# Attention of layer 1 in a two-layer decoder trunk: other distances between the steps of a head group, nine early pieces of the output projection, table loads only at a change of set

## The chip, the cores and the metric

The kernel runs on one core of a Trainium2 chip. The metric is the device time of one execution in microseconds; lower is better. DVE is VectorE, ACT is ScalarE, PE is TensorE, PEld its weight loads, SP the engine that issues the weight transfers.

## The reference

Two layers over 256 positions, width 2048, all in float32. Layer 0 mixes with gated DeltaNet heads and RG-LRU channels, layer 1 with banded attention; each layer then has cross attention to 256 memory tokens and a gated feed-forward part. What the change touches is the mixer of layer 1:

```
q, k, v = split(h @ swa_in_w)           # 32 query heads, 8 key/value heads, 64 wide
q = rope(rmsnorm(q) * q_norm);  k = rope(rmsnorm(k) * k_norm)
s = q k^T / 8 over the own and the previous block of 128, masked to a band of 128
m = max(max(s), sink);  p = exp(s - m) / (sum(exp(s - m)) + exp(sink - m))
x = x + (p v) @ swa_out_w
```

## The kernel before, in words

All weights stream once from memory, in 800 pieces of 512 x 256 numbers. A piece goes through four steps: a transfer into `w_raw` (SP), a cast to its high part `w_hi` on ACT (`split`, L475), the rest `w_lo` on DVE (`split`, L875), and 24 matmuls of 128x256 on PE (`piece`, L1460 to L1462; in the feed-forward input `wide_piece`). Each buffer holds four pieces, and ACT and DVE split three pieces ahead (`AHEAD`): in tick t they split piece t + 3, and that cast waits until PE has done piece t - 1. Four pieces give a group of 256 output columns.

Each engine has its own program, written by hand as a list of ticks. A tick is one piece and after it (on PE) or after its split (on ACT and DVE) the other work of this tick. Engines meet only through semaphores, and each runs its list strictly in order. So the order on every engine, and with it what waits behind what, is set by the tick at which a step is put.

In layer 1 the keys and values take 16 ticks (`SWKV`) and the queries 32 (`SWQ`), four ticks for one group g of four query heads. The attention of group g is a chain of steps at ticks 4g + lag (`swa_first`, `swa_side`, `rope`):

| step of group g | engine, line | lag before | lag after |
|---|---|---|---|
| take the group out of PSUM, square | DVE L884, ACT L541 | 3 | 3 |
| sum over the head | PE L1690 | 4 | 4, behind the scores |
| table load, logarithm, exponential (root) | ACT L478, L548, L549 | 4 | 4, mostly no load |
| refine the root, normalise ("normalising") | DVE L888 to L890, L1339 | 5 | 5 |
| rotation matmul | PE L1866 | 6 | 7 |
| last step of the rotation | DVE L1343 to L1345 | 6 | 7, ahead of L884 |
| scores | PE L1907, L1908 | 7 | 8 |
| mask and maxima | DVE L1371 to L1384 | 7 | 8 |
| exponentials | ACT L805 to L807 | 8, ahead of the root | 9 |
| scale by the row sums ("scaling") | DVE L1352 to L1355 | 9, ahead of the split | 10, behind it |
| transposes | PE L1444 | 10 | 11 |
| copies of them | ACT L823 | 10 | 11 |
| product with V | PE L1890 to L1892 | 11 | 12 |
| split of the output into `act` ("output split") | DVE L901, L902 | 12 | 13 |

The steps of the last groups run on into the output projection (`common(1)`, `mixout`). Its piece (g, q) needs the attention of the groups up to 2q + 1. `mix_order` and `EARLY` give the order of its first pieces: those that need the last groups least come first. A group's accumulator lies in one of two banks by turns (`ST`); a third one can lie in bank `B[1]`, which is free once the last queries are rotated.

`tables(name)` on ACT loads a set of activation tables, at every call. Logarithm and exponential are in one set, which `head_rstd`, `row_rstd` and parts of layer 0's mixer ask for; in layer 0's projection the chain at tick 9 is: sums on PE (L1561), load, four table functions (L573 to L576), cast, `w_lo`, then `q_buf`, `k_buf`, `k_dec` on DVE (L1028 to L1033) for the matmuls of tick 11 (L1554).

Of the kernel before, what the change touches and what calls it, by code (L numbers as in the profile page):

```python
# [80 lines left out]
EARLY = [(0, 0), (0, 1), (0, 2), (1, 0), (1, 1), (1, 2), (0, 3), (1, 3)]  # L81
# [11 lines left out]
def mix_order(layer, t):  # L93

    return EARLY[t] if layer and t < 8 else (t // 4, t % 4)

# [73 lines left out]
def trunk(nc, a, out):  # L170
    ctx = ExitStack()
    with ctx:
# [287 lines left out]
        def _(act):  # L460
# [15 lines left out]

            def tables(name):
                nc.scalar.preload_act_table_set(name)  # L478
# [218 lines left out]
            def common(layer):  # L697
# [7 lines left out]
                if layer == 1:  # L705
                    for t in range(32, 41):
                        if t < 38:
                            mixout(t - 32)
                        swa_first(t)
                        swa_side(t)  # L710
                    first = 6
# [87 lines left out]
            def swa_first(t):  # L799

                g = (t - 8) // 4
                if 8 <= t and g < 8 and t == 4 * g + 8:
                    act.wait_ge(s_neg, g + 1)
                    for i in range(4):
                        f(sc[:, i, 0:P], sc[:, i, 0:P], ACT.Exp, bias=sst[:, 1, i:i + 1], accum_out=sst[:, 2, i:i + 1])  # L805
                        f(sc[:, i, P:384], sc[:, i, P:384], ACT.Exp, bias=sst[:, 1, 4 + i:5 + i], accum_out=sst[:, 2, 4 + i:5 + i])  # L806
                    f(sst[:, 4, :], sst[:, 3, :], ACT.Exp).then_inc(s_exp, 1)  # L807

            def swa_side(t):

                g = (t - 3) // 4
                if 3 <= t and g < 8 and t - 4 * g == 3:
                    swa_rope(N_ROPE + 2 + g, GROUP[SWQ] + g, 3)
                g = (t - 4) // 4
                if 4 <= t and g < 8 and t == 4 * g + 4:
                    swa_rope(N_ROPE + 2 + g, 0, 4)
                g = (t - 10) // 4
                if 10 <= t and g < 8 and t == 4 * g + 10:
# [5 lines left out]
                    last.then_inc(pt_copied, 1)  # L824

# [14 lines left out]
            for t in range(16):  # L840
# [6 lines left out]
                if t in (7, 11):  # L847
                    act.wait_ge(ksw_done, g)
                    nc.scalar.copy(kTs[:, 2 * (g - 1):2 * g, :], B[2][:].rearrange("p (k c) -> p k c", k=2)).then_inc(ksw_ready, 1)
                if t == 12:  # L850
                    act.wait_ge(svT, 1)
                    nc.scalar.copy(vtok[:, :, 0:2, :], B[0][:].rearrange("p (t k c) -> p t k c", t=TT, k=2)).then_inc(sv_ready, 1)
            for t in range(32):
                split(SWQ + t + AHEAD)
                swa_first(t)
# [584 lines left out]
        def _(pe):  # L1440
# [492 lines left out]
            for t in range(16):  # L1933
# [12 lines left out]
                if t == 12:  # L1946
                    swa_v(0)
# [27 lines left out]
```

## Time and profile before

| | |
|---|---|
| times of three runs | 2801.35, 2809.43, 2815.41 us; median 2809.43 |
| profiled execution: time, span | 2811.95 us, 2809.8 us |
| mean granted clock of PE | 0.975 of full |
| chain that ended last, by engine | PE 82%, DVE 10%, ACT 5%, issue 2%, DMA 1% |
| table loads | 54, 69.3 us on ACT |
| keys and queries of layer 1 up to the first late piece of the output projection | about 1595 to 1884 us |

The span is that of the instructions on the core, the time that of the whole execution. The clock row is the mean of what the chip granted to PE: full speed is 2.4 GHz, half is 1.2.

### The profile page before, as it was taken

Reading aid. Unit: us, or ns where it says so; the run is one execution under the profiler, and the core shown is the slowest. Engines: PE = TensorE matmul, PEld = TensorE weight load, DVE = VectorE, ACT = ScalarE, POOL = GpSimd, SP = SyncE. Lnnn points to the kernel's source line nnn. Section 1 sums busy time; section 2 is a strip of 40 time slices with the busy share of each in tenths; the row PEclk is TensorE's granted clock in tenths of the full one; section 3 lists DMA queues with packets and bytes.
Section 4 is the critical chain, followed back from the end, with each engine's and each line's share of the span. In section 5 each row is a group of like instructions: output and inputs, shape, how many; then the busy total and the mean of one; then the engine's idle time right before and its main releaser. Section 6 shows DMA issues by size and latency. Waiting matters only on the chain.

```text
span 2809.8 us, 46427 instructions
## 1 busy us (share of the span) xinstructions
PE 2658.7 (95%) x18376; PEld 2455.4 (87%) x18376; DVE 1789.3 (64%) x2468; ACT 1169.4 (42%) x1490; POOL 10.0 (0%) x18
## 2 busy tenths in 40 slices
PE   6898998899899999999999998789899999999999
PEld 5798898899898899889989886679788998899889
DVE  4666666655777755775576656655577746764774
ACT  2434434444444433443444444433444434443443
POOL 0000000000000000000000000000000000000000
PEclk8999999999999999999999999889899999999999
DMA  5343443355446655565555442225256655665554
GB/s 149 99 120 99 114 119 108 111 167 163 144 146 188 192 186 180 184 189 187 181 185 180 152 128 83 76 80 172 87 166 193 189 184 173 189 193 184 183 182 155
DMA packets 429633, 432.62 MB, mean 154 GB/s; under 512 B 15487, under 2 KB 427796, under 8 KB 429108
## 3 DMA queue, kind: packets, MB, share of 16 engines
q1 hardware_dynamic: 422832, 422.63, 48.6%
q0 software_dynamic: 1584, 5.40, 0.7%
q10 hardware_dynamic: 5076, 2.56, 0.3%
q8 instruction: 107, 1.75, 0.3%
q14 instruction: 34, 0.28, 0.0%
HBM read 428.44 MB, written 2.10 MB: 153 GB/s over the span
## 4 chain that ended last, share of the span: by engine, by line
PE 82%; DVE 10%; ACT 5%; issue 2%; DMA 1%; SPq 0%; ACTq 0%; POOL 0%; DVEq 0%
PE stream L1475 23%; PE stream L1460 13%; PE stream L1461 12%; PE stream L1462 12%; PE stream L1476 12%; DVE w_lo L875 2%; PE bank L1554 1%; ACT w_hi L475 1%; PE bank L1495 1%; ACT L478 1%; PE bank L1444 1%; PE bank L1866 1%; PE stream L1554 1%; DMA cst<-in_consts 1%; ACT scores L806 0%
## 5 line engine op out<-in xcount | busy, mean ns | idle before, releaser
L875 DVE TENSOR_TENSOR w_lo<-w_raw,w_hi 128x1024 fp32r<-128x1024 f32 x800 | 965.8, 1222 | 585.8 <-ACT w_hi L475 582.3
L475 ACT CAST w_hi<-w_raw 128x1024 fp32r<-128x1024 f32 x800 | 833.9, 1047 | 822.0 <-PE stream L1462 481.0
L1475 PE MATMUL stream<-h,w_hi 128*128 128x512 f32 x2816 | 992.2, 398 | 0.0
L1476 PE MATMUL stream<-h,w_lo 128*128 128x256 f32 x2816 | 788.9, 280 | 0.0
L1475 PEld LDWEIGHTS stream<-h,w_hi 128*128 128x128 f32 x2816 | 529.0, 188 | 130.2
L1460 PE MATMUL stream<-act,w_hi 128*128 128x256 f32 x2048 | 589.6, 288 | 2.6 <-DVE act L902 2.5
L1462 PE MATMUL stream<-act,w_lo 128*128 128x256 f32 x2048 | 581.1, 284 | 0.0
L1461 PE MATMUL stream<-act,w_hi 128*128 128x256 f32 x2048 | 581.1, 284 | 0.0
L1476 PEld LDWEIGHTS stream<-h,w_lo 128*128 128x128 f32 x2816 | 531.4, 189 | 0.1
L1460 PE MATMUL stream<-h,w_hi 128*128 128x256 f32 x1536 | 472.8, 308 | 3.0 <-DVE w_lo L875 3.0
L1461 PE MATMUL stream<-h,w_hi 128*128 128x256 f32 x1536 | 444.5, 289 | 0.0
L1462 PE MATMUL stream<-h,w_lo 128*128 128x256 f32 x1536 | 443.7, 289 | 0.0
L1460 PEld LDWEIGHTS stream<-act,w_hi 128*128 128x128 f32 x2048 | 394.8, 193 | 6.5 <-DVE act L902 3.9
L1461 PEld LDWEIGHTS stream<-act,w_hi 128*128 128x128 f32 x2048 | 394.6, 193 | 1.6 <-issue 0.8
L1462 PEld LDWEIGHTS stream<-act,w_lo 128*128 128x128 f32 x2048 | 394.5, 193 | 0.0
L1460 PEld LDWEIGHTS stream<-h,w_hi 128*128 128x128 f32 x1536 | 306.2, 199 | 19.1 <-issue 15.3
L1461 PEld LDWEIGHTS stream<-h,w_hi 128*128 128x128 f32 x1536 | 305.5, 199 | 10.1 <-issue 9.6
L1462 PEld LDWEIGHTS stream<-h,w_lo 128*128 128x128 f32 x1536 | 304.6, 198 | 0.0
L1231 DVE TENSOR_TENSOR ffn_cross<-stream,ffn_cross 128x512 f32<-128x512 f32 x88 | 60.9, 692 | 99.0 <-ACT ffn_cross L765 99.0
L765 ACT COPY ffn_cross<-stream 128x512 f32<-128x512 f32 x88 | 51.6, 587 | 155.4 <-PE stream L1476 155.4
L478 ACT ACT_TABLE_LOAD x54 | 69.3, 1283 | 60.7 <-PE bank L1600 29.8
L929 DVE SCALAR_TENSOR_TENSOR ffn_conv<-ffn_pad,par,ffn_conv 128x256 f32<-128x256 f32 x176 | 77.6, 482 | 13.1 <-DVE ffn_conv L923 6.7
(332 smaller groups left out, 1741.0 us busy)
## 6 DMA issues: line engine op xcount, KB each, us to landing
w_raw<-in_ffn_in_w SPq DMA_DIRECT2D x352, 512.0 KB, 4.5
w_raw<-in_ffn_out_w SPq DMA_DIRECT2D x176, 512.0 KB, 3.6
w_raw<-in_hyb_in_w SPq DMA_DIRECT2D x96, 512.0 KB, 3.8
w_raw<-in_swa_in_w SPq DMA_DIRECT2D x48, 512.0 KB, 3.5
w_raw<-in_xkv_w SPq DMA_DIRECT2D x32, 512.0 KB, 3.5
w_raw<-in_hyb_out_w SPq DMA_DIRECT2D x32, 512.0 KB, 3.5
w_raw<-in_swa_out_w SPq DMA_DIRECT2D x32, 512.0 KB, 3.4
w_raw<-in_xq_w SPq DMA_DIRECT2D x16, 512.0 KB, 3.5
```

What stands on the lines that cost most here:

```text
L475: nc.scalar.copy(whi[:, k], raw[:, n % NRAW]).then_inc(hi_split, 1)
L478: nc.scalar.preload_act_table_set(name)
L765: nc.scalar.copy(two(frt[:, t // 4]), wide(g0 + t // 4)[:, :, TOK:512]).then_inc(ffn_right, 1)
L875: v.tensor_tensor(wlo[:, k], raw[:, n % NRAW], whi[:, k].bitcast(F32), ALU.subtract).then_inc(lo_split, 1)
L929: last = v.scalar_tensor_tensor(d, pad[:, b, j:j + TOK], par[:, col(j, b)], d, ALU.mult, ALU.add)
L1231: v.tensor_tensor(two(frt[:, t // 4]), both[:, :, 0:TOK], two(frt[:, t // 4]), ALU.add).then_inc(group_evac, 1)
L1460: mm(o, whi[:, k, kk, w], src[:, kt, 0, :], start=first, stop=False, skip_group_check=True)
L1461: mm(o, whi[:, k, kk, w], src[:, kt, 1, :], start=False, stop=False, skip_group_check=True)
L1462: last = mm(o, wlo[:, k, kk, w], src[:, kt, 0, :], start=False, stop=final, skip_group_check=True)
L1475: mm(bank[:, m, :], whi[:, k, kk, w], h[:, kt, :, :], start=(q == 0 and kk == 0), stop=False, skip_group_check=True)
L1476: last = mm(bank[:, m, 0:TOK], wlo[:, k, kk, w], h[:, kt, 0, :], start=False, stop=(q == 3 and kk == len(kts) - 1), skip_group_check=True)
L1554: last = mm(bank[:, s], lhs[:, s], rhs if rhs.shape[1] == P else rhs[:, s], start=True, stop=True)
```

## The change

The attention steps after the normalising move one tick later each, in the keys' ticks too, and change their order within a tick; the row scaling goes behind the split and ahead of the next mask. `EARLY` takes nine pieces of three groups instead of six of two, the third group in `B[1]`. The tail of the attention runs to tick 41 instead of 40. `tables` loads only if the name differs from the last one: 26 loads instead of 54.

```diff
-EARLY = [(0, 0), (0, 1), (0, 2), (1, 0), (1, 1), (1, 2), (0, 3), (1, 3)]
+EARLY = [(g, q) for g in range(3) for q in range(3)] + [(g, 3) for g in range(3)]
+SWA_LAST = 42
...
             def tables(name):
-                nc.scalar.preload_act_table_set(name)
+                if loaded[0] != name:
+                    nc.scalar.preload_act_table_set(name)
+                loaded[0] = name
...
             def swa_side(t):
+                for lag in (7, 3, 5):
+                    g = (t - lag) // 4
+                    if t >= lag and g < 8 and t == 4 * g + lag:
+                        if lag == 7 and g:
+                            dve.wait_ge(s_done, g)
+                        rope(lag, N_ROPE + 2 + g, GROUP[SWQ] + g, SWQ + t, two(qf[:]), "swa_q_norm", q_rot)
+                g = (t - 10) // 4
+                if t >= 10 and g < 8 and t == 4 * g + 10:
                     dve.wait_ge(s_exp, g + 1)
...
-                g = (t - 7) // 4
-                if 7 <= t and g < 8 and t == 4 * g + 7:
+                g = (t - 8) // 4
+                if t >= 8 and g < 8 and t == 4 * g + 8:
                     dve.wait_ge(s_done, g + 1)
...
-                if t == 6:
+                if t == 7:
                     pe.wait_ge(n_out, ni + 1)
                     mm(B[1][:], c_("rot"), nraw[:], start=True, stop=True).then_inc(rot_done, 1)
...
-                    piece(MIXOUT[layer] + t, GROUP[MIXOUT[layer]] + g, q, 3, act_, range(NK * q, NK * q + NK))
+                    third = layer and g == 2
+                    if third and q == 0:
+                        pe.wait_ge(q_rot, 8)
+                    piece(MIXOUT[layer] + t, GROUP[MIXOUT[layer]] + g, q, 3, act_, range(NK * q, NK * q + NK), B[1] if third else None)
...
-                g = (t - 12) // 4
-                if 12 <= t and g < 8 and t == 4 * g + 12:
+                g = (t - 13) // 4
+                if t >= 13 and t == 4 * g + 13:
                     dve.wait_ge(pv_done, g + 1)
```

First place: DVE in the middle of the queries, from the `w_lo` behind the maxima on. The names are tiles, `softmax_small` and `scores` of the scaling, `norm_sq`, `norm_r`, `norm_raw` of the next group's normalising, `act` the output split. Before:

```order
L875 TENSOR_TENSOR w_lo<-w_raw,w_hi 128x1024
L901 CAST act<-stream 128x2x256
L902 TENSOR_TENSOR act<-stream,act 128x2x256
L1352 TENSOR_TENSOR softmax_small<-softmax_small 128x8
L1353 RECIPROCAL softmax_small<-softmax_small 128x8
L1354 TENSOR_TENSOR scores<-scores,softmax_small 128x4x128
L1355 TENSOR_TENSOR scores<-scores,softmax_small 128x4x256
L875 TENSOR_TENSOR w_lo<-w_raw,w_hi 128x1024
L888 SCALAR_TENSOR_TENSOR norm_sq<-bank,norm_r 128x512
L889 SCALAR_TENSOR_TENSOR norm_sq<-norm_sq,norm_r 128x512
L890 SCALAR_TENSOR_TENSOR norm_r<-norm_sq,norm_r 128x512
L1339 SCALAR_TENSOR_TENSOR norm_raw<-norm_raw,par,norm_r 128x512
```

The change:

```order
L875 TENSOR_TENSOR w_lo<-w_raw,w_hi 128x1024
L888 SCALAR_TENSOR_TENSOR norm_sq<-bank,norm_r 128x512
L889 SCALAR_TENSOR_TENSOR norm_sq<-norm_sq,norm_r 128x512
L890 SCALAR_TENSOR_TENSOR norm_r<-norm_sq,norm_r 128x512
L1339 SCALAR_TENSOR_TENSOR norm_raw<-norm_raw,par,norm_r 128x512
L901 CAST act<-stream 128x2x256
L902 TENSOR_TENSOR act<-stream,act 128x2x256
L875 TENSOR_TENSOR w_lo<-w_raw,w_hi 128x1024
L1357 TENSOR_TENSOR softmax_small<-softmax_small 128x8
L1358 RECIPROCAL softmax_small<-softmax_small 128x8
L1359 TENSOR_TENSOR scores<-scores,softmax_small 128x4x128
L1360 TENSOR_TENSOR scores<-scores,softmax_small 128x4x256
```

The normalising and the output split now both stand ahead of the scaling, and the `w_lo` that stood between scaling and normalising is now ahead of the scaling.

Second place: ACT in the same turn, from the end of the exponentials (`softmax_small`) on; `norm_r` is the root, `probsT` the copies of the transposes, `norm_sq` the square of a new group. Before:

```order
L807 ACTIVATE softmax_small<-softmax_small 128x8
L478 ACT_TABLE_LOAD
L548 ACTIVATE norm_r<-bank,bias_consts 128x512
L549 ACTIVATE norm_r<-norm_r 128x512
L475 CAST w_hi<-w_raw 128x1024 x2
L823 COPY probsT<-bank 128x512 x2
L823 COPY probsT<-stream 128x512
L475 CAST w_hi<-w_raw 128x1024
L541 ACTIVATE norm_sq<-norm_raw 128x512
L475 CAST w_hi<-w_raw 128x1024
```

The change:

```order
L825 ACTIVATE softmax_small<-softmax_small 128x8
L476 CAST w_hi<-w_raw 128x1024 x2
L811 COPY probsT<-bank 128x512 x2
L811 COPY probsT<-stream 128x512
L546 ACTIVATE norm_sq<-norm_raw 128x512
L476 CAST w_hi<-w_raw 128x1024
L553 ACTIVATE norm_r<-bank,bias_consts 128x512
L554 ACTIVATE norm_r<-norm_r 128x512
L476 CAST w_hi<-w_raw 128x1024
```

The root has moved from ahead of the copies to behind the square, and the load in front of it is gone.

Third place: DVE in the keys' ticks, from the normalising of a key group on. Before:

```order
L1339 SCALAR_TENSOR_TENSOR norm_raw<-norm_raw,par,norm_r 128x512
L875 TENSOR_TENSOR w_lo<-w_raw,w_hi 128x1024
L1343 TENSOR_TENSOR norm_sq<-bank,sin 128x512
L1344 TENSOR_TENSOR norm_raw<-norm_raw,cos 128x512
L1345 TENSOR_TENSOR kT<-norm_raw,norm_sq 128x512
L875 TENSOR_TENSOR w_lo<-w_raw,w_hi 128x1024
L884 TENSOR_TENSOR norm_raw<-stream,rstd 128x512
```

The change:

```order
L1339 SCALAR_TENSOR_TENSOR norm_raw<-norm_raw,par,norm_r 128x512
L875 TENSOR_TENSOR w_lo<-w_raw,w_hi 128x1024 x2
L1343 TENSOR_TENSOR norm_sq<-bank,sin 128x512
L1344 TENSOR_TENSOR norm_raw<-norm_raw,cos 128x512
L1345 TENSOR_TENSOR kT<-norm_raw,norm_sq 128x512
L884 TENSOR_TENSOR norm_raw<-stream,rstd 128x512
```

The last step of the rotation (`kT`) has moved behind one more `w_lo` and now stands directly ahead of the next group's `norm_raw`.

## Rows read from the trace of the kernel before

**Rows 1.** The page's first part: busy time, share of the span, instructions.
```profile
PE 2658.7 (95%) x18376; PEld 2455.4 (87%) x18376; DVE 1789.3 (64%) x2468; ACT 1169.4 (42%) x1490; POOL 10.0 (0%) x18
```

**Rows 2.** Waits of TensorE, 1590 to 1890: line waited for, total us, times, longest.
```profile
PE bank L1866 <- DVE norm_raw L1339: 33.2, 10, 3.9
PE bank L1444 <- DVE scores L1355: 9.9, 8, 4.5
PE stream L1890 <- ACT probsT L823: 1.7, 1, 1.7
PE stream L1460 <- DVE act L902: 1.5, 1, 1.5
```

**Rows 3.** Windows: length, busy of PE, PEld, DVE, ACT, POOL; clock, DMA share, GB/s.
```profile
1595.50:1648.00 52.50, 48.45 (x347) 44.79 (x346) 28.99 (x33) 21.18 (x25) 0.00 (x0) 0.93 0.50 157
1685.40:1711.70 26.30, 21.56 (x152) 18.65 (x152) 17.73 (x26) 12.17 (x29) 0.00 (x0) 0.94 0.27 81
...
1738.00:1765.40 27.40, 22.68 (x152) 19.56 (x152) 17.73 (x26) 12.11 (x29) 0.00 (x0) 0.88 0.26 77
```

**Rows 4.** Timeline of TensorE, one turn: start, length, what [idle before, releaser].
```profile
1737.97 1.09 PE L1444 MATMUL bank<-cst,scores 128*128 128x128 f32 x8 [0.82 <-DVE scores L1355]
...
1743.38 2.07 PE L1866 MATMUL bank<-norm_raw,cst 128*128 128x512 f32 x2 [3.88 <-DVE norm_raw L1339]
...
1750.01 0.43 PE L1890 MATMUL stream<-probsT,v_tok 128*64 128x128 f32 x2
...
1751.74 0.48 PE L1907 MATMUL bank<-kT_swapped,q_rot 64*128 64x128 f32 x2
...
1757.85 1.02 PE L1690 MATMUL bank<-norm_sq,cst 128*128 128x512 f32 x2
```

**Rows 5.** Timeline of DVE, the same turn.
```profile
1735.65 0.17 DVE L1352 TENSOR_TENSOR softmax_small<-softmax_small 128x8 f32<-128x8 f32 x1 [1.32 <-ACT softmax_small L807]
...
1740.40 0.68 DVE L888 SCALAR_TENSOR_TENSOR norm_sq<-bank,norm_r 128x512 f32<-128x512 f32 x1
...
1754.98 0.69 DVE L1371 SCALAR_TENSOR_TENSOR scores<-bank,cst 128x512 f32<-128x512 f32 x1 [4.10 <-PE stream L1908]
...
1759.24 1.22 DVE L875 TENSOR_TENSOR w_lo<-w_raw,w_hi 128x1024 fp32r<-128x1024 f32 x1
1760.38 0.68 DVE L901 CAST act<-stream 128x512 fp32r<-128x512 f32 x1
```

**Rows 6.** Timeline of ACT, the same turn.
```profile
1731.90 0.41 ACT L805 ACTIVATE scores<-scores,softmax_small 128x128 f32<-128x128 f32 x1 [6.88 <-DVE softmax_small L1384]
...
1735.64 1.28 ACT L478 ACT_TABLE_LOAD   x1
...
1738.19 1.98 ACT L475 CAST w_hi<-w_raw 128x1024 fp32r<-128x1024 f32 x2
```

**Rows 7.** Instructions of line 478: duration ns min, median, max, first and last start.
```profile
L478 ACT ACT_TABLE_LOAD  x54: 1283/1283/1283, 40.9 to 2056.8; - x54
```

**Rows 8.** Layer 0's projection: waits of TensorE; timelines of ACT and DVE.
```profile
PE bank L1554 <- DVE k_dec L1033: 9.5, 4, 2.4
...
446.06 1.28 ACT L478 ACT_TABLE_LOAD   x1 [0.22 <-PE bank L1561]
...
450.87 1.22 DVE L875 TENSOR_TENSOR w_lo<-w_raw,w_hi 128x1024 fp32r<-128x1024 f32 x1 [2.12 <-ACT w_hi L475]
```

**Rows 9.** Windows of one microsecond, columns as in rows 3.
```profile
223.00:224.00 1.00, 1.00 (x10) 1.00 (x9) 0.74 (x1) 0.00 (x0) 0.00 (x0) 0.78 0.82 289
...
454.00:455.00 1.00, 0.84 (x7) 0.84 (x8) 1.00 (x2) 0.00 (x0) 0.00 (x0) 1.00 1.00 348
1991.00:1992.00 1.00, 1.00 (x5) 0.83 (x6) 0.93 (x1) 0.00 (x0) 0.00 (x0) 0.83 0.01 3
```

**Rows 10.** Layer 1's cross attention: timelines of TensorE and DVE.
```profile
1990.85 3.03 PE L1714 MATMUL bank<-kv_mem,xq 128*128 128x256 f32 x8 [2.02 <-DVE xq L1188]
...
2003.74 0.69 DVE L888 SCALAR_TENSOR_TENSOR norm_sq<-bank,norm_r 128x512 f32<-128x512 f32 x1 [0.83 <-ACT norm_r L549]
```

More of the change, by code:

```diff
@@ L93, in mix_order @@
 def mix_order(layer, t):
-    return EARLY[t] if layer and t < 8 else (t // 4, t % 4)
+    return EARLY[t] if layer and t < len(EARLY) else (t // 4, t % 4)
 CONST = {}
@@ L797, in swa_rope @@
                     head_rstd(ni, B[0][:], nr[:], SWA_HD)
[L799 to L807, printed above, removed]
-            def swa_side(t):
[L811 to L818, printed above, removed]
+            def swa_side(t):
+                g = (t - 11) // 4
+                if t >= 11 and t == 4 * g + 11:
                     act.wait_ge(pt_done, g + 1)
@@ L824, in swa_side @@
                     last.then_inc(pt_copied, 1)
+                g = (t - 3) // 4
+                if g < 8 and t == 4 * g + 3:
+                    swa_rope(N_ROPE + 2 + g, GROUP[SWQ] + g, 3)
+                g = (t - 4) // 4
+                if t >= 4 and g < 8 and t == 4 * g + 4:
+                    swa_rope(N_ROPE + 2 + g, 0, 4)
+                g = (t - 9) // 4
+                if t >= 9 and g < 8 and t == 4 * g + 9:
+                    act.wait_ge(s_neg, g + 1)
+                    for i in range(4):
+                        f(sc[:, i, 0:P], sc[:, i, 0:P], ACT.Exp, bias=sst[:, 1, i:i + 1], accum_out=sst[:, 2, i:i + 1])
+                        f(sc[:, i, P:384], sc[:, i, P:384], ACT.Exp, bias=sst[:, 1, 4 + i:5 + i], accum_out=sst[:, 2, 4 + i:5 + i])
+                    f(sst[:, 4, :], sst[:, 3, :], ACT.Exp).then_inc(s_exp, 1)
             for t in range(16):
@@ L854, in _ @@
                 split(SWQ + t + AHEAD)
-                swa_first(t)
                 if t == 0:
@@ L1259, in mixout @@
                     if q == 3:
-                        residual(GROUP[MIXOUT[layer]] + g, g, MIXOUT[layer] + t, "norm_cross", KT * layer)
+                        residual(GROUP[MIXOUT[layer]] + g, g, MIXOUT[layer] + t, "norm_cross", KT * layer,
+                                 B[1] if layer and g == 2 else None)
                 first = 0
                 if layer == 1:
-                    for t in range(32, 41):
-                        swa_first(t)
-                        if t < 38:
+                    for t in range(32, SWA_LAST):
+                        if t < 41:
                             mixout(t - 32)
                         swa_side(t)
-                    first = 6
+                    first = 9
                 for t in range(first, 32):
@@ L1763, in common @@
                         mem_side(0, 16)
-                    g = {7: 0, 8: 1}.get(t) if layer and t <= 8 else t // 4 - 1 if t % 4 == 0 and t else None
+                    g = {10: 0, 11: 1, 12: 2}.get(t) if layer and t <= 12 else t // 4 - 1 if t % 4 == 0 and t else None
                     if g is not None:
```

84 lines of the change are left out of this document (39 added, 45 removed).

## The prediction, made before the change was run

> **What bounds the kernel now.** The page's first part comes first: TensorE is busy 95% of the span [rows 1]. So time can only come from its 5% of idle, from stretches at half clock, or from other engines where they make it wait. The waits of TensorE in the stretch of layer 1's attention (1590 to 1890 us) say where [rows 2]. It waits 33.2 us in 10 places for the normalised heads ahead of the rotation (L1866), 9.9 us in 8 places for the scaled scores ahead of their transposes (L1444), and 1.7 and 1.5 us at the end. Seven of the ten L1866 waits are 3.88 (queries 1 to 7), which leaves 2.0 for each of the other three (two groups of keys, first group of queries). So the eight groups of queries with their end hold 33.2 - 6.1 + 9.9 + 1.7 + 1.5 = 40.2 us of waiting.
>
> The windows by group give the second loss, the clock [rows 3]. A group takes 26.3 us at a mean clock of 0.94 or 27.4 at 0.88. At half of full clock work takes twice as long, so (1 - clock) x length is lost: 1.6 or 3.3 us. I take 2.9 for the latter, since part of that low stretch falls into the wait itself. Two groups lose 1.6 and six (the last with the end) about 2.9: 20.6 us.
>
> The timelines of the three engines give one turn of the loop, counted from the end of the scores of a group (DVE starts the mask at 1754.98) [rows 4 to 6]. TensorE: a piece until 1757.85, so 2.9; head sum 1.0; transposes 1737.97 to 1739.50 (the wait's 3.88 ahead of 1743.38), so 1.5; rotation about 1.0 at full clock; product with V 1750.01 to 1751.74, 1.7; scores until the mask at 1754.98, 3.2. DVE: mask, maxima 1754.98 to 1759.24, 4.3; w_lo 1.14; normalising 1740.40 to the rotation at 1743.38, 2.9 and the hand-over; output split two operations of 0.68, 1.4; scaling 1735.65 to the transposes at 1737.97, 2.3; last step of the rotation three operations of this size (0.69, as at 1754.98), 2.0. ACT: exponentials 1731.90 to 1735.64, 3.75; table load 1.28; logarithm and exponential until 1738.19, 1.3; a cast 1.0.
>
> The old loop checks this. Mask, exponentials, scaling: 4.3 + 3.75 + 2.3 = 10.4. From 1737.97 to 1740.40 DVE waits for a cast that sits behind the table load and does a w_lo, 2.4, then the normalising, 3.0. Then rotation, piece, V, scores: 1.0 + 2.9 + 1.7 + 3.2 = 8.8. Sum 24.6; with 1.6 or 2.9 of clock 26.2 or 27.5. The windows show 26.3 and 27.4 [rows 3].
>
> **The change, part by part.**
>
> *Table loads.* 54 loads become 26; each of the 54 took 1283 ns, although most load the set that is in place [rows 7]. Of the 28 removed, those count that end a wait of TensorE. In layer 0's projection TensorE waits 2.4 us four times for k_dec [rows 8]. The load at 446.06 starts as soon as TensorE's sums are there, then come four table functions and the cast, and DVE has waited 2.12 for that cast at 450.87. All of it moves up by the load: 4 x 1.28 = 5.1. Two of these four waits were followed by half clock (at 223 us, and so in the third pair), two were not (454 us) [rows 9]. A rest of 1.1 should bring none, 2 x 1.7 = 3.4 more. In layer 1's cross attention the wait of 2.02 at 1990.85 shrinks by 1.28, and the fall of the clock at 1991 (1.7, [rows 9]) should go too; the next chain gains only the 0.8 for which DVE waited for ACT at 2003.74 [rows 10]. Together 3.8. The other removed loads lie beside running pieces: 0; a cover gone would show as a wait ahead of a piece.
>
> The Trainium skill (ScalarE: Activation LUTs, "What ACT_TABLE_LOAD costs") puts 1283 ns plus a drain of about 1380 ns on each switch to another set. By the rows load, logarithm and exponential together take 2.55 (1735.64 to the casts at 1738.19) [rows 6], which leaves no room for such a drain; by the page the four places would give up to their whole wait, 9.5 instead of 5.1.
>
> *Rotation a step later (keys and first queries).* TensorE reaches the rotation after one more piece, 2.9 against a wait of 2.0: all 6.1 us go, and the half clock that followed two of them: 0.93 over 52.5 us is 3.7 lost [rows 3], of which I take 3.4. New: the evacuation of the next group now stands behind the rotation's last step on DVE. The square on ACT (0.63) then ends 2.0 + 0.7 + 0.6 = 3.3 after the rotation, TensorE asks for it after one piece, 2.9: 0.5 lost, once. Sum 9.0. Later groups have the scores in between and lose nothing.
>
> *The queries' loop.* New order on DVE from the end of the scores: mask 4.3, w_lo 1.14, normalising 2.9 (its input from ACT is there at 1.0 + 1.3 = 2.3, wanted at 5.4), output split 1.4, w_lo 1.14 (its cast is behind the exponentials, 4.3 + 3.75 + 1.0 = 9.1, wanted at 9.7), scaling 2.3. The transposes can start at 13.2. TensorE has 1.0 + 3 x 2.9 = 9.7 of work, so it waits 3.5. The rotation behind them no longer waits, since its input was ready at 8.3. From there 1.5 + 1.0 + 2.9 + 1.7 + 3.2 = 10.3: a turn of 23.5 against 24.6. On DVE behind the scaling: w_lo, rotation's last step, evacuation, w_lo; the last waits for its cast, which stands behind square and copies on ACT. It ends about 21.1, so 2.4 of room before the mask at 23.5. On ACT the head's square ends about 18.9, wanted at 23.5.
>
> The waits of the eight groups: group 0 has no output split, but then DVE waits for the cast: 12.6 - 9.7 = 2.9. Groups 1 to 5: 5 x 3.5 = 17.5. Group 6: the third mix-output piece (1, or (0,2)) is the first to need the output split of group 5, which DVE reaches at 9.8, while TensorE is there after 1.0 + 2.9: a wait of 5.9, and none at its transposes. Group 7: no normalising, scaling done at 12.6; TensorE has three pieces, 8.7: 3.9. That is where the pieces of the early third group lie: they fill what were waits of 4.5 and 1.7 with nothing in them. At the end one more output split: 1.5. Sum 31.7 against 40.2: 8.5 gained.
>
> The clock behind these waits was not seen for this arrangement. A wait of 3.88 was followed by one low stretch (1.7) twice and by two (2.9) five times [rows 3]. Those had a shorter wait and the transposes ahead of them, which here stand behind. I take 2.2 for each of six, and 5.6 for group 6 and the end: 18.8 against 20.6, 1.8 gained; the bounds are 1.7 and 2.9 for each of the six (15.8 and 23.0): +4.8 to -2.4.
>
> The Trainium skill (TensorE: Matmul & The Clock Gate, "Part 4: PE-mode transpose") says that transposes do not count as busy for the clock the way matmuls do, which speaks against this order. By it, wait and transposes are one quiet stretch of 5.0, each group loses 2.9, and the loop gains 6.1 instead of 10.3.
>
> *Sum.* 5.1 + 3.4 + 3.8 + 9.0 + 8.5 + 1.8 = 31.6 us. The profiled execution took 2811.95 for its span of 2809.8, so 2780 there. The median of the three runs is 2.5 lower, 2809.4; I forecast 2779.
>
> **The rivals.** Half a per cent, 14 us, is about what a measurement of this kernel tells from no change.
>
> 1. The forecast, a gain of 24 to 40 us: 2770 to 2786. Chance 0.60.
> 2. The queries' loop gives nothing: DVE's work in front of the scaling (4.3 + 1.14 + 2.9 + 1.4 + 1.14 = 10.9, where mask and exponentials took 8.1) leaves a turn only 1.1 us shorter, and more falls of the clock in two steps, or hand-overs that I left out of the walk, eat that. For it: five of seven such waits had two steps. Against: one of the two waits of a turn goes whole. 31.6 - 10.3 = 21.3, or 18 if the clock of layer 0 stays as it is: 2788 to 2792. Chance 0.22.
> 3. Loads and loop give nothing, the chains being held by something else that comes at the same time; only the steps of the keys are left, 9.0: 2800. Against: DVE's wait for the cast is 2.12 long in the row. Chance 0.09.
> 4. More than 40 us, if most falls of the clock behind 3.5 us go: 2760 to 2769. Chance 0.04.
> 5. Slower, over 2823. The normalising now stands ahead of the scaling on DVE's queue and waits for ACT's root of the next group. If that is late, the scaling, the transposes and the whole turn are late. It has 5.4 - 2.3 = 3.1 us of room. To undo the 21 us made elsewhere and lose 14 more, seven turns must each lose 6.5 against my walk (35 + 10.3 over seven): the root 9.6 us late. ACT's work ahead of it (copies, square, cast) ends 4 us before it is wanted. Chance 0.05.
>
> Within 0.5%: rival 3 and a tenth of rival 2, 0.11. Slower 0.05, faster the rest, 0.84. The range 2762 to 2800 takes in cases 1, 2 and most of 4.
>
> **What the profile after would show.** Table loads 26. L1866's waits for norm_raw gone (under 1 us in all). TensorE's wait for the scaled scores longest with 3.5 in six groups, starts of those transposes 25 to 26.5 apart instead of 27.4. A wait of about 5.9 ahead of a piece for DVE's act. k_dec's wait 4 x 1.1. The window 1600 to 1648 at a clock near 1. The forecast is wrong if the transposes stay 27 apart, if w_lo turns up as a releaser of TensorE, or if new falls of the clock appear where there was none.

## The result and the profile after

The changed kernel takes 2777.77 us (median of 4 runs, 2772.21 to 2782.40) against 2809.76 for the kernel before on the same chip (4 runs, 2801.35 to 2815.41): ratio 0.988, interval 0.985 to 0.991. Timed again beside the experiments it took 2776.19, ratio 0.986 (0.983 to 0.989). The forecast was 2779.

So the gain was 32.0 us the first time and 40.3 us the second (2816.53 - 2776.19). The profiled executions, 2811.95 and 2772.21, lie 39.7 us apart, since the one after is the fastest of its four. I use its rows for places and shapes, and keep the second profile of the same kernel (2776.19, span 2772.9) beside it where a size matters.

The page's first two lines of after, to be read with [rows 1]:

```profile
span 2770.0 us, 46406 instructions
...
PE 2643.6 (95%) x18376; PEld 2446.2 (88%) x18376; DVE 1788.6 (65%) x2468; ACT 1134.3 (41%) x1462; POOL 10.0 (0%) x18
```

The same 18376 matmuls are there. Span minus busy time gives TensorE's idle time: 151.1 before (2809.8 - 2658.7), 126.4 after. So, between the two profiles, 24.7 us less is waiting, and 15.1 us less is matmuls that ran for less time. These are the two terms of the forecast, waits (21.3) and clock (10.3), read for the whole kernel from one row. I use this ledger for every experiment.

One part of the 15.1 has nothing to do with the change. Count the matmuls in order of their starts: from the 5601st to the 6801st (828.9 to 1029.1 us before) TensorE never waits and the granted clock is 1.00, yet they took 200.2 us before and 196.9 after. The two profiles of the loads-only kernel below, one and the same program, show 200.2 and 196.9 as well. So 3.3 us of TensorE's busy time come and go between executions; why is open.

The waits of TensorE from 1560 to 1895, the stretch of [rows 2]:

```profile
PE bank L1440 <- DVE scores L1360: 23.4, 7, 3.7
PE stream L1456 <- DVE act L902: 7.3, 2, 5.8
...
PE bank L1686 <- issue: 1.0, 1, 1.0
```

No row names `norm_raw` any more: where it cost 33.2 us, the transposes now wait 23.4. One turn of the loop on the three engines, to be laid beside [rows 4 to 6] (start, length, what, idle time before it and its releaser). TensorE:

```profile
1717.79 1.97 PE L1440 MATMUL bank<-cst,scores 128*128 128x128 f32 x8 [3.36 <-DVE scores L1360]
...
1720.40 1.91 PE L1865 MATMUL bank<-norm_raw,cst 128*128 128x512 f32 x2
...
1743.68 1.71 PE L1440 MATMUL bank<-cst,scores 128*128 128x128 f32 x8 [3.36 <-DVE scores L1360]
...
1815.52 0.58 PE L1456 MATMUL stream<-act,w_hi 128*128 128x256 f32 x1 [5.81 <-DVE act L902]
...
1845.56 1.22 PE L1440 MATMUL bank<-cst,scores 128*128 128x128 f32 x8 [3.74 <-DVE scores L1360]
```

DVE and ACT in the same turn:

```profile
1730.67 0.69 DVE L1368 SCALAR_TENSOR_TENSOR scores<-bank,cst 128x512 f32<-128x512 f32 x1 [2.66 <-PE stream L1908]
...
1736.07 0.68 DVE L888 SCALAR_TENSOR_TENSOR norm_sq<-bank,norm_r 128x512 f32<-128x512 f32 x1
...
1742.41 1.22 DVE L1360 TENSOR_TENSOR scores<-scores,softmax_small 128x1024 f32<-128x1024 f32 x1
...
1731.73 0.69 ACT L553 ACTIVATE norm_r<-bank,bias_consts 128x512 f32<-128x512 f32 x1 [4.97 <-PE bank L1686]
```

The mask starts at 1730.67 and the transposes at 1743.68, 13.0 apart (walked: 13.2). Between them DVE never waits: no instruction of it from 1731.28 to 1742.41 has a bracket, the two shown at 1736.07 and 1742.41 among them. The root is taken at 1731.73, 1.1 after the mask starts, so rival 5 (a late root in front of the scaling) has its 3 us of room. The waits of 5.81 and 3.74 are those walked for groups 6 and 7.

The turns by windows, with the columns of [rows 3]; the clock is the first figure behind POOL:

```profile
1584.00:1636.50 52.50, 51.45 (x400) 48.39 (x399) 31.00 (x35) 23.36 (x27) 0.00 (x0) 1.00 0.58 176
1693.16:1717.79 24.63, 21.21 (x152) 18.82 (x153) 17.64 (x27) 10.99 (x27) 0.00 (x0) 0.92 0.27 85
1717.79:1743.68 25.89, 22.47 (x152) 19.60 (x153) 17.64 (x27) 11.00 (x27) 0.00 (x0) 0.89 0.27 84
1743.68:1768.53 24.85, 21.43 (x153) 18.72 (x153) 17.64 (x27) 10.99 (x27) 0.00 (x0) 0.92 0.27 85
1768.53:1793.02 24.49, 21.07 (x153) 18.76 (x153) 17.63 (x27) 10.99 (x27) 0.00 (x0) 0.92 0.28 86
```

The keys (first row) run at full clock; before they had 0.93. The turn ahead of the four had no low stretch and took 23.17 us (transposes at 1669.99 and 1693.16; walked: 23.5). The four shown took 24.5 to 25.9, so the half clock cost each of them 1.3 to 2.7 us.

In layer 0 the waits for `k_dec` and the loads:

```profile
PE bank L1550 <- DVE k_dec L1033: 3.3, 3, 1.1
...
L482 ACT ACT_TABLE_LOAD x26 | 33.4, 1283 | 38.7 <-PE bank L1596 29.8 <-DVE angle L1413 4.0 <-PE bank L1491 3.2
```

9.5 in four [rows 8] are now 3.3 in three, and 54 loads [rows 7] are 26. The second profile has all four waits:

```profile
PE bank L1550 <- DVE k_dec L1033: 4.4, 4, 1.1
```

The clock behind the two of these waits that half clock had followed, in windows of 5 us from the end of the wait. Before:

```profile
222.66:227.66 5.00, 5.00 (x30) 5.00 (x31) 1.08 (x1) 0.00 (x0) 0.00 (x0) 0.66 0.60 186
339.20:344.20 5.00, 5.00 (x30) 5.00 (x31) 1.07 (x1) 0.00 (x0) 0.00 (x0) 0.66 0.61 188
```

After:

```profile
223.73:228.73 5.00, 5.00 (x44) 5.00 (x45) 2.20 (x5) 0.00 (x0) 0.00 (x0) 1.00 0.60 182
335.90:340.90 5.00, 5.00 (x44) 5.00 (x45) 2.21 (x5) 0.00 (x0) 0.00 (x0) 1.00 0.62 191
```

### The profile page after: what moved, and what is told of

The parts are those of the page before. It is cut to its first block and busy times, and to the rows that moved or that the text cites. A ratio compares the mean times of both kernels' runs of the same rounds, so it can differ in the third digit from the quotient of the medians.

```text
span 2770.0 us, 46406 instructions
## 1 busy us (share of the span) xinstructions
PE 2643.6 (95%) x18376; PEld 2446.2 (88%) x18376; DVE 1788.6 (65%) x2468; ACT 1134.3 (41%) x1462; POOL 10.0 (0%) x18
## 5 line engine op out<-in xcount | busy, mean ns | idle before, releaser
L1456 PE MATMUL stream<-act,w_hi 128*128 128x256 f32 x2016 | 581.0, 288 | 8.3 <-DVE act L902 8.3
L1458 PE MATMUL stream<-act,w_lo 128*128 128x256 f32 x2016 | 572.3, 284 | 0.0
L1457 PE MATMUL stream<-act,w_hi 128*128 128x256 f32 x2016 | 572.3, 284 | 0.0
L1456 PE MATMUL stream<-h,w_hi 128*128 128x256 f32 x1536 | 464.7, 303 | 3.0 <-DVE w_lo L875 3.0
L1457 PE MATMUL stream<-h,w_hi 128*128 128x256 f32 x1536 | 439.9, 286 | 0.0
L1456 PEld LDWEIGHTS stream<-act,w_hi 128*128 128x128 f32 x2016 | 389.0, 193 | 11.9 <-DVE act L902 9.5
L1457 PEld LDWEIGHTS stream<-act,w_hi 128*128 128x128 f32 x2016 | 388.8, 193 | 1.8 <-issue 1.0
L1458 PEld LDWEIGHTS stream<-act,w_lo 128*128 128x128 f32 x2016 | 388.6, 193 | 0.0
L1456 PEld LDWEIGHTS stream<-h,w_hi 128*128 128x128 f32 x1536 | 301.2, 196 | 15.7 <-issue 11.9
L1193 DVE TENSOR_TENSOR xT<-stream,xT 128x512 f32<-128x512 f32 x79 | 54.6, 691 | 47.3 <-PE stream L1458 47.2
```

The costliest lines, as they stand in the source:

```text
L1193: v.tensor_tensor(x2, two(ST[gi % 2] if bank is None else bank), x2, ALU.add).then_inc(group_evac, 1)
L1456: mm(o, whi[:, k, kk, w], src[:, kt, 0, :], start=first, stop=False, skip_group_check=True)
L1457: mm(o, whi[:, k, kk, w], src[:, kt, 1, :], start=False, stop=False, skip_group_check=True)
L1458: last = mm(o, wlo[:, k, kk, w], src[:, kt, 0, :], start=False, stop=final, skip_group_check=True)
```

## The experiments

They ran in three sets, each beside the kernel before on the same chip (2815.66, 2816.53 and 2812.25 us; 15, 11 and 11 runs). "Idle" and "busy" are TensorE's, against 151.1 and 2658.7 before, from the first two lines of each page. They come from one execution each, and the kernel before has one profile only: two profiles of one kernel differ by up to 3 us in them, and medians are safer for totals. Where two kernels of different sets are compared, I compare what each gained on the kernel before of its own set, since that reference moved by 4 us.

| kernel | median us | ratio (interval) | idle | busy |
|---|---|---|---|---|
| the change, again | 2776.19 | 0.986 (0.983 to 0.989) | -22.1 | -14.8 |
| loads only | 2768.99 | 0.983 (0.982 to 0.984) | -23.2 | -19.8 |
| loads only, again | 2768.27 | 0.984 (0.981 to 0.986) | -21.3 | -22.8 |
| the queries' 7 loads only | 2782.15 | 0.989 (0.987 to 0.992) | -9.4 | -17.2 |
| steps only | 2794.00 | 0.993 (0.991 to 0.994) | -7.2 | -10.8 |
| keys' step only | 2808.02 | 0.997 (0.996 to 0.998) | -0.4 | -1.5 |
| loads and keys' step | 2765.62 | 0.984 (0.981 to 0.986) | -23.5 | -15.9 |
| the change, old early list | 2776.62 | 0.986 (0.985 to 0.988) | -20.4 | -16.3 |
| the change, other early order | 2773.46 | 0.985 (0.983 to 0.988) | -25.2 | -17.2 |
| that, scaling first | 2738.43 | 0.973 (0.971 to 0.976) | -46.8 | -32.0 |
| scaling first, all loads | 2751.62 | 0.980 (0.977 to 0.983) | -31.3 | -30.1 |
| scaling first, output split ahead of it | 2752.91 | 0.979 (0.976 to 0.982) | -35.7 | -23.4 |

### The two halves of the change

Loads only is the kernel before with the memory of the last set:

```diff
             def tables(name):
-                nc.scalar.preload_act_table_set(name)
+                if loaded[0] != name:
+                    nc.scalar.preload_act_table_set(name)
+                loaded[0] = name
```

> The kernel before with the table loads only at a change of set (54 loads become 26), nothing else. Theory A: loads cost wherever ACT's chain is what TensorE waits for, and in the old order of the queries' loop that holds in every turn, since the cast for which DVE waits ahead of the normalising stands behind the load: 7 x 1.3, plus 3 x 1.3 at the rotations of the keys and of the first queries, plus 5.1 in layer 0's projection, plus 2.1 in the cross attention: about 20 us, 2788 to 2792, and the wait for norm_raw falls from 33.2 to about 20. Theory B (the account of the prediction, which counts the loads outside the loop alone and gives the loop to the steps): 5.1 + 3.8, up to 3.4 of clock, 2797 to 2802. Theory C: loads are hidden everywhere, no change.

Steps only is the changed kernel with a load at every call again.

> The changed kernel with a table load at every call again (54). Theory A: in the new order the load of a turn stands on ACT where nothing waits for it, so the keys give 9 and the queries' loop and the end 10 as walked: 2788 to 2792, and the two halves of the change add up to more than the whole (32 us). Theory B: the halves add up, 32 less what the loads give alone (9 to 12): 2786 to 2789. If the load does end a wait in the new loop, turns of more than 25 us between transposes: 2795 or more.

The loads alone make 2768.99, below everything that was expected of them and below the whole change. The expected waits came (23.2 us less idle, against about 20); what no theory had is the 19.8 us of matmul time. The steps alone make 2794.00, above both theories (2786 to 2792) and just under the mark for a load that ends a wait in the new loop. The waits of the loads-only kernel from 1560 to 1895:

```profile
PE bank L1870 <- DVE norm_raw L1343: 20.6, 10, 2.5
PE bank L1448 <- DVE scores L1359: 9.9, 8, 4.5
```

33.2 has become 20.6. A turn there, on ACT and DVE:

```profile
1714.49 0.19 ACT L811 ACTIVATE softmax_small<-softmax_small 128x8 f32<-128x8 f32 x1
1714.59 0.67 ACT L552 ACTIVATE norm_r<-bank,bias_consts 128x512 f32<-128x512 f32 x1
...
1715.76 1.22 DVE L1359 TENSOR_TENSOR scores<-scores,softmax_small 128x1024 f32<-128x1024 f32 x1
1716.90 1.22 DVE L879 TENSOR_TENSOR w_lo<-w_raw,w_hi 128x1024 fp32r<-128x1024 f32 x1
1718.03 0.68 DVE L892 SCALAR_TENSOR_TENSOR norm_sq<-bank,norm_r 128x512 f32<-128x512 f32 x1
```

The root follows the exponentials at once, and `w_lo` and the normalising follow the scaling without a gap. Before, load, root and cast ended behind the scaling, and DVE stood 1.34 us in front of that `w_lo`:

```profile
1739.26 1.23 DVE L875 TENSOR_TENSOR w_lo<-w_raw,w_hi 128x1024 fp32r<-128x1024 f32 x1 [1.34 <-ACT w_hi L475]
```

So the load in the loop was on the path: it is in the 2.4 us from 1737.97 to 1740.40 of the old walk, and TensorE's wait of 3.88 is 2.44 without it.

Both were run again in one set, to see whether loads only really beats the change.

> The kernel before with table loads only at a change of set once more, beside the changed kernel. Theory A: 0.983 again, some 10 to 15 us below the changed kernel, because the old order without the load has turns of 25.0 (a wait of 2.5 ahead of the rotation, seldom followed by half clock), the new one turns of 24.5 to 25.9 and a wait of 5.8 at the end. Theory B: the same time as the changed kernel within 0.3%.

> The changed kernel once more, on the chip and in the rounds of the next three. Theory A (the steps of the queries' loop take back a part of what the loads give): ratio to the kernel before about 0.988, clearly above the loads alone. Theory B (the kernel with the loads alone came out low by its run): both within 0.3% of each other.

It does, by 7.9 us (2768.27 against 2776.19). That is less than the 10 to 15 of theory A and, at 0.29%, just inside the 0.3% of theory B, so the two expectations don't decide it. The single times do better: all six of loads only lie below four of the change's five. In the first set the loads-only kernel (2764.20 to 2771.91) also lies wholly below the change with its old early list (2772.79 to 2779.13). The ledger says where: the idle time is the same (-21.3 and -22.1), the busy time is 8.0 us lower. The steps of the change thus cost nothing in waiting on top of the loads, and 8 us in matmul time.

### The loads of the queries alone

The kernel before, with no load at the roots of queries 1 to 7:

```diff
             def head_rstd(ni, bank, dst, width):
...
-                tables(LN_EXP)
+                if not 9 <= ni <= 15:
+                    tables(LN_EXP)
```

> The kernel before without the seven table loads of queries 1 to 7; the other 47 stay. Theory: each turn loses the 1.3 us for which DVE waited for the cast behind the load, 9.4 in all, and the shorter wait ahead of the rotation (2.5 instead of 3.9) is followed by fewer low stretches, 20.6 down to 8 to 11 of clock: 19 to 22 us, half of what all 28 loads give. Rival (the loads matter outside the loop): 9 us or less.

Seven loads, 9.0 us of ACT's time, are worth 30.1 us by the medians (23 to 37 by the interval), where 19 to 22 were expected. The waits for `norm_raw` fall from 33.2 to 23.2, which is 7 times 1.44, and that is the 9.4 of idle time. Busy time is 17.2 less, but not all of it belongs to these loads. By windows of one microsecond the queries lose 12.2 us less to half clock (20.6 to 8.4), which with the waits makes 22, as expected. Another 5.3 us is in the cross attention (8.6 to 3.3), whose loads this kernel leaves in place, and counts as chance.

```profile
PE bank L1867 <- DVE norm_raw L1340: 23.2, 10, 2.4
```

Now the change can be added up, roughly. Loads alone give 46.7 us (48.3 the second time), of which the loop has 22 to 30, so the others give 17 to 25. The steps alone give 21.7. Together 39 to 47, where the change measured 32.0 and 40.3 in its two timings. With the new steps the loop's loads are nearly hidden: the transposes' waits are 25.6 with them and 23.4 without, 0.4 per turn.

### The keys' step alone

The keys' rotation a tick later and ahead of the evacuation, nothing else:

```diff
-                if t in (6, 10):
-                    rope(6, N_ROPE + g - 1)
                 if t in (7, 11):
-                    pe.wait_ge(kT_done, g)
+                    rope(7, N_ROPE + g - 1)
+                if t in (8, 12):
+                    pe.wait_ge(kT_done, g - 1)
```

> The kernel before with the rotation of the two key groups and what follows it one tick later, as in the change; queries and table loads as before. Theory: two waits of 2.0 go, 3.4 of half clock go, 0.5 comes: 6.9 us less, 2802 to 2804, the window 1600 to 1648 of the old kernel at a clock of 1. Rival: the evacuation behind the rotation's last step costs more than it gives: no gain, and a wait ahead of the second group's head sum.

> Table loads only at a change of set, and the keys' rotation a tick later (e1 and e3 together), queries as before. Theory: without the loads the two keys' waits are 2.0 and 0.7, so the keys' step now gives 2.7 less 0.5 and at most one low stretch of the clock: 2 to 4 us less than the loads alone, 2764 to 2767. Rival: the gain of e3 (8) adds in full, 2760.

Alone it gives 7.6 us, where 6.9 was walked. On top of the loads it gives nothing that can be measured: the kernel gains 46.6 us on its own reference, the loads alone 46.7 and 48.3, though the median is 2.7 us lower and inside the 2764 to 2767 expected. That fits: with the loads gone the three waits of 2.0 are already down to 2.02, 0.74 and 0.74. In the profile of the keys' step alone the waits for `norm_raw` are 29.1 in 8, so two of the three are gone; the third belongs to the first queries, which this kernel leaves as they were. One wait of 1.0 is new, at the second key group's head sum. The keys thus wait 3.1 us less and lose 1.7 less to the clock (3.4 to 1.7), 4.8 of the 7.6; one of the two low stretches stays. The table's -0.4 hides the waits, since this profile has 3.1 us more idle time ahead of 400 us, where the edit changes nothing.

### The early pieces

The changed kernel with the old list and no third group:

```diff
-EARLY = [(g, q) for g in range(3) for q in range(3)] + [(g, 3) for g in range(3)]
+EARLY = [(0, 0), (0, 1), (0, 2), (1, 0), (1, 1), (1, 2), (0, 3), (1, 3)]
...
-                    third = layer and g == 2
+                    third = False
```

> The changed kernel with the old list of early pieces (six pieces of two groups, no third bank). Theory: after the last scores TensorE has one piece instead of three ahead of the last transposes, so their wait grows from 3.7 to about 9.5, and the product with V waits 1.7 for the copies again: 7.5 us more than the changed kernel, 2784 to 2787. Rival: the three pieces only move from the end to the middle and the end is bound by DVE anyway: same as the changed kernel, 2778.

2776.62: the third group changes nothing that can be measured in the total, as the rival had it. Its waits do come back (7.4 at the last transposes, where about 9.5 was walked, and 1.7 for the last copies; 27.1 + 1.7 against 23.4), 5.4 us more. From 1560 to 1895 us TensorE is idle 41.1 us, against 35.8 and 35.6 in the two profiles of the change, so nothing is given back there. The ledger hides it: the second profile of the change has 2.6 us more idle time ahead of 480 us, and both lose 4 us more to the clock in the cross attention (8.5 and 8.7 against 4.5), places that the list doesn't touch. An effect of 5 us is as large as such differences.

Then the order in which no piece needs group 5's output early:

```diff
-EARLY = [(g, q) for g in range(3) for q in range(3)] + [(g, 3) for g in range(3)]
+EARLY = [(0, 0), (0, 1), (1, 0), (1, 1), (0, 2), (1, 2), (2, 0), (2, 1), (2, 2)] + [(g, 3) for g in range(3)]
```

> The changed kernel with the early pieces in another order: (0,0) (0,1) (1,0) (1,1) (0,2) (1,2) (2,0) (2,1) (2,2), so that the first piece that needs the output split of group 5 comes two ticks later. Theory: the wait of 5.8 for DVE's act goes, the transposes of group 6 wait 3.4 like the others instead of not at all: 2.4 us less than the changed kernel, and one low stretch of the clock less, 2 to 5 us in all. Rival: no difference, if a wait of 3.4 costs as much clock as one of 5.8.

The wait of 5.81 is gone, the transposes of group 6 wait their 3.4 instead, and the time is 2.7 us lower. That is within what was expected, but the intervals of the two ratios overlap, so it isn't shown.

### Scaling first

In the other early order, the scaling goes back ahead of its tick's split, and the output split goes a tick later, behind it:

```diff
             for t in range(32):
+                swa_first(t)
                 split(SWQ + t + AHEAD)
...
-                g = (t - 13) // 4
-                if t >= 13 and t == 4 * g + 13:
+                g = 7 if t == 41 else (t - 14) // 4
+                if t >= 14 and (t == 41 or t == 4 * g + 14):
                     dve.wait_ge(pv_done, g + 1)
```

`swa_first` holds only the scaling, lag 10.

> The early order of e5, and on DVE the scaling ahead of the w_lo of its tick and the output split one tick later (behind the scaling). Theory: DVE's work between mask and scaling is then w_lo and normalising alone, the scaling is done at 10.6 instead of 13.2 after the scores, TensorE waits 0.9 per turn instead of 3.4, turns are 21 us, half clock in the queries goes nearly whole: 7 x 2.5 + 8 to 13 of clock less than e5, 2740 to 2750. Rival: the scaling waits for the exponentials on ACT (cast ahead of them late), or the later output split is waited for by the product with V: turns of 23 or more, 2760 to 2770.

2738.43 us, the fastest kernel of this study, 38 us below the change and just under the 2740 to 2750 expected. DVE now does `w_lo`, normalising, scaling after the mask, and 2.5 us less (one `w_lo`, one output split) stands ahead of the transposes. Its waits, and two of its turns by windows:

```profile
PE bank L1444 <- DVE scores L1355: 8.0, 8, 1.7
```

```profile
1685.88:1706.58 20.70, 19.73 (x153) 17.42 (x153) 17.55 (x27) 11.00 (x27) 0.00 (x0) 1.00 0.33 102
1706.58:1727.28 20.70, 19.73 (x153) 17.42 (x153) 17.55 (x27) 11.00 (x27) 0.00 (x0) 1.00 0.33 103
```

A turn is 20.7 instead of 24.5 to 25.9, with 0.91 us of waiting ahead of the transposes and no half clock from 1560 to 1895. Against its parent (2773.46) it gains 35 us: 21.6 of idle time and 14.8 of busy time.

Which of its two edits does it? Output split at lag 13 again, ahead of the scaling:

> The kernel of e6 with the output split back in its tick of the change (ahead of the scaling), so that against e5 only the w_lo and the scaling have changed places. Theory: scaling done 1.14 earlier and no longer behind the cast: 12.0 after the scores, a wait of 2.3 per turn; turns of 22.5 to 23.5: 8 us of waits and some clock less than e5, 2756 to 2762. Rival: the order of scaling and w_lo alone brings all of e6, 2740.

And the same fast order with a load at every call:

> The kernel of e6 (scaling ahead of the w_lo, output split behind it, later early pieces) with a table load at every call again. Theory: in this order the load of a turn stands on ACT two ticks before DVE wants the root, so only layer 0's projection (5.1), the cross attention (2.1) and some clock come back: 2746 to 2752. Rival: the load delays the cast or the exponentials of the turn, 8 x 1.3 more: 2758 or more.

Both do. By the medians, moving the scaling ahead of `w_lo` is worth 20.6 us (2773.46 to 2752.91) and moving the output split behind it 14.5 more. By the gains on each set's own reference (43.1, 59.3 and 78.1) it is 16.3 and 18.8. So each part is known to some 5 us, and which is the larger isn't shown. The kernel in between came out below the 2756 to 2762 expected. Here are two neighbouring turns of the variant with the output split ahead, from transposes to transposes, each begun by a wait of 2.23 us:

```profile
1690.85:1712.89 22.04, 19.75 (x153) 17.45 (x153) 17.64 (x27) 11.00 (x27) 0.00 (x0) 1.00 0.30 96
1712.89:1736.51 23.62, 21.34 (x153) 18.48 (x153) 17.64 (x27) 10.99 (x27) 0.00 (x0) 0.93 0.28 90
```

One stays at full clock, the other falls and takes 1.6 us more. The loads, put back into the fast order, cost 13.2 us by the medians (2751.62, within what was expected) and 17.5 by the gains on each reference (78.1 against 60.6). The profiles put that into idle time (15.5 more, and 1.9 more busy), mostly outside the loop: the transposes' waits are 10.9 against 8.0, 0.4 per turn.

## Why the prediction was right, and where its reading was wrong

The terms of the sum, against the profile after. Clock is found from windows of one microsecond, (1 - clock) times busy time. By these windows the whole kernel lost 62.6 us before and 51.9 after, 10.7 less where the busy time fell by 15.1. Of the difference of 4.4 us, 3.3 is the stretch from 828.9 to 1029.1 told above, and 1.1 I can't place.

| term | forecast | measured |
|---|---|---|
| `k_dec` waits | 5.1 | 6.2 (9.5 to 3.3); second profile 5.1 (9.5 to 4.4) |
| clock there (200 to 480 us) | 3.4 | 3.5 (10.2 to 6.7); second profile 3.4 |
| clock from 97 to 200 us | 0 | -3.3 (3.1 to 6.4); second profile -0.1 |
| cross attention of layer 1, waits | 2.1 | 1.6 (`xq` 6.3 to 4.1, `x_probs` 4.0 to 4.6) |
| clock there | 1.7 | 0 (8.6 both times) |
| keys and first queries, waits | 5.6 | 5.1 |
| clock there | 3.4 | 3.4 |
| queries' loop, waits | 8.5 | 9.5 (40.2 to 30.7) |
| clock there | 1.8 | 6.9 (20.6 to 13.7); second profile 2.5 |
| layer 0's normalised `h` | not seen | 1.2 (4.6 to 3.4) |

**The waits.** 21.3 forecast, 23.6 found in places and 24.7 in the ledger. The walk through the loop holds to 0.2 us at every wait that it named: 3.36 for 3.5, 2.89 for 2.9 at group 0, 5.81 for 5.9, 3.74 for 3.9, 1.51 for 1.5. It was made of durations from one turn and the order on each engine, and nothing else. At the keys the new wait was 1.0 where 0.5 was walked. The one term not seen is a load ahead of layer 0's cross attention, at TensorE's wait for `h`.

**The clock.** The parts in layer 0 and at the keys came as forecast. With the waits for `k_dec` at 1.1, both low stretches behind them are gone. From 200 to 480 us the five kernels with all loads there lose 10.2 to 11.9 us, the nine without the repeated ones 6.6 to 6.8. A fall elsewhere can hide this: from 97 to 200 us, behind waits that the change leaves as they were, the first profile has 3.3 us more, the second 0.1. The cross attention gave none of its 1.7: the waits for `xq` and `x_probs` that remain (longest 3.4 and 2.8) were followed by as much half clock as before (8.6, then 8.5 and 8.7). The loop gained 6.9 in one profile and 2.5 in another of the same kernel, where 1.8 was forecast. That is the size of chance in this term.

**The number.** That it came so near is in part luck. The sum taken from the median gives 2809.4 - 31.6 = 2777.8, not the 2779 written; 2777.77 was measured. But the second timing gained 40.3 us on its reference, just over the 24 to 40 of the forecast's case, so the gain is known to some 4 us either way. Of the signs named, the starts of the transposes came 24.5 to 25.9 apart (25 to 26.5 forecast), and new falls of the clock did appear, at 132 and 470 us in the first profile and at 357 in the second, behind waits of 1.9 that the change doesn't touch. They were called a sign of being wrong, and are chance.

The forecast price for the loads in layer 0 came from the rows, one load less at each place, and that is what happened: waits of 2.4 became waits of 1.1. The Trainium skill (ScalarE: Activation LUTs, "What ACT_TABLE_LOAD costs") adds a drain to each switch to another set; the forecast had worked out that with it these waits could go whole. The 3.3 and 4.4 us left speak against it here, though the loads removed repeat a set and are no switches. A load that does switch shows no such drain either; ahead of the keys the set changes from the sine's, and the next function starts 0.02 us behind the load:

```profile
1588.65 1.28 ACT L482 ACT_TABLE_LOAD   x1 [1.41 <-PE bank L1686]
1589.95 0.69 ACT L553 ACTIVATE norm_r<-bank,bias_consts 128x512 f32<-128x512 f32 x1
```

The loop gained 12 to 16 us, waits and clock, in the two profiles, where the forecast had 6.1 if its transposes were part of a quiet stretch. That was the rule of the Trainium skill (TensorE: Matmul & The Clock Gate, "Part 4: PE-mode transpose"), by which transposes don't count as busy in the way matmuls do. Directly behind a wait of 0.91, the same transposes left the clock at 1.00; no run here has a long wait without transposes behind it in the new order, so the rule itself is not tested.

**The step that failed** is "The other removed loads lie beside running pieces: 0". For the loop of the changed kernel it nearly holds, 2.2 us of waits. All 28 loads put back into that kernel cost 18.6 us, though (gains of 21.7 against 40.3), where the sum had 12.3 for them. And as a reading of the old kernel it is wrong: seven of those loads gave 30.1 us, some 22 of it in rows of the loop. The old-loop check had the evidence in it, "From 1737.97 to 1740.40 DVE waits for a cast that sits behind the table load and does a w_lo, 2.4", and I did not draw the line from that to the load's price. The consequence is that the gain was put to the wrong half. The forecast gave the steps 19.3 us and the loads 12.3; run alone the steps give 21.7 and the loads 46.7. In the loop the two halves gain the same microseconds: both take the load out of the path to `norm_raw`, one by removing it and one by moving the root. So the whole, at 40.3 (32.0 in the first timing), is 28 less than the sum of its parts, and the steps on top of the loads are a loss of 7.9 us.

Why a loss, when idle time is equal? The steps put the whole waiting of a turn in one place, 3.4 in front of the transposes, where loads alone leave two waits of 0.8 and 2.44. A wait of 3.36 was followed by half clock in ten of ten turns of the two profiles. In loads only, the wait of 2.44 was followed by it in six of fourteen. Here are three neighbouring turns of its first profile, from transposes to transposes:

```profile
1692.14:1717.03 24.89, 21.58 (x152) 18.64 (x152) 17.64 (x27) 10.88 (x28) 0.00 (x0) 0.93 0.27 85
1717.03:1740.36 23.33, 20.01 (x153) 17.45 (x153) 17.56 (x27) 10.89 (x28) 0.00 (x0) 1.00 0.29 91
1740.36:1765.25 24.89, 21.58 (x153) 18.47 (x153) 17.64 (x27) 10.88 (x28) 0.00 (x0) 0.93 0.27 86
```

At full clock the turn is 23.33 us, against 23.17 in the changed kernel: the orders differ in the clock, not in the work or the waits.

From 1560 to 1895 the loads-only kernel loses 7.7 and 6.1 us to the clock in its two profiles, the changed kernel 13.7 and 18.1: 6 to 12 us more, which holds the 8. Four more kernels agree. The steps with all loads and with the old list lose 15.8 and 18.3; the old order of the queries without the loop's loads loses 10.1 and, with the keys' step, 11.9. The scaling-first kernels carry the same line further, now ahead of the same transposes. Waits of 2.2 were followed by half clock in four of six turns and lose 6.7 in the queries, waits of 0.9 lose nothing. So the length matters; whether the place of the wait, ahead of the transposes or of the rotation, matters as well isn't separated. That it is the queries' loop, and not the keys' step or the early list, goes by exclusion: with the keys' step the loads keep their gain, and both other lists stay slower than loads only.

**Open.** From 560 to 827 us, layer 0's middle, measured from the same matmul to the same matmul, the changed kernel is 4.2 and 3.2 us faster in its two profiles. Shorter waits make 2.5 of the first (1.2 for `h`, 1.5 for a transfer of the memory tokens, less 0.2) and a fall of the clock that is gone makes 1.6 more; whether the transfer's part belongs to the loads wasn't tried. Open are the 3.3 us between 828.9 and 1029.1 us, what the third early group's 5.4 us of waits are worth in the median, and where the loads cost the rest of their 18.6 us in the new order.

## What to carry to other kernels

When two edits of one change both relieve the same chain, price each one alone against the old kernel as well as both together: a step that a walk shows waiting behind an instruction has already said what that instruction costs. Walk the order of each engine with durations from one turn; here it gave every wait of the loop to 0.2 us, and the same walk led to the order that is 38 us faster still: on the engine that TensorE waits for, put what TensorE waits for ahead of what it doesn't. With TensorE 95% busy, judge an order by how its idle time is cut up, not by the sum alone: here equal waiting in long pieces cost 8 us more than in short ones. And a price for half clock wants more than one profile.

## What the hardware showed that was not expected

- A wait of the same length can be followed by half clock or not. In the queries' loop it followed 3.36 us in ten of ten turns, 2.44 us in six of fourteen (loads only, two profiles), 2.23 us in four of six (output split ahead of the scaling) and 0.91 us in none of six (scaling first). In the profile with 2.23, two neighbouring turns have clock 1.00 and 0.93.
- Removing 9.0 us of loads from ACT, an engine that is busy 42% of the span, took 30.1 us off the kernel by the medians; the rows of its loop show 22, of which 10 is waiting and 12 half clock that followed the waits.
- Two profiles of one kernel gave the queries 13.7 and 18.1 us of lost clock with all waits equal to 0.1 us, so a clock term is known only to some 5 us from one profile.
- The same 1200 matmuls, with no wait among them and the granted clock at 1.00, took 200.2 us in six of the fourteen profiles and 196.9 us in eight. Both values occur for one and the same kernel, so 3.3 us of a difference between two profiles can be this alone.
- All 54 loads took 1283 ns, repeated sets and switches alike.
